# V stage: the low parts of the gates of 30 of 32 quads subtracted on GpSimd, between its gathers

## What is computed

```python
def block(args):
    xb, eb, gb = args
    u = jnp.take(u_tab, eb, axis=0)
    act = jax.nn.gelu(jnp.einsum("cd,ced->ce", xb, u))
    vv = jnp.take(v_tab, eb, axis=0)
    return jnp.einsum("ce,ced->cd", gb * act, vv)
```

## Time and profile before

| what | value |
|---|---|
| median of 3 runs | 1966.7 us (1954.4 to 1967.1) |
| the profiled execution | 1962.9 us |
| its span, first to last instruction | 1961.1 us |
| busy PE, DVE, ACT, POOL | 97%, 80%, 49%, 27% of the span |
| V stage, first to last dense matmul | 1471.3 to 1949.6 us |
| VectorE's loop with gathers, first to last | 1482.4 to 1945.9 us |

### The profile page before, as it was taken

One profiled execution on the slowest core, in us unless ns is written; L12 is line 12 of the kernel. 1 busy time (PEld: TensorE's weight loads), 2 busy tenths in 40 slices (PEclk: granted clock), 3 DMA queues, 4 the chain that ended last, 5 costly groups with the idle time before them and its releaser, 6 DMA issues.

```text
span 1961.1 us, 34213 instructions
## 1 busy us (share of the span) xinstructions
PE 1906.1 (97%) x13424; PEld 1678.9 (86%) x13424; DVE 1561.5 (80%) x2398; ACT 965.0 (49%) x1387; POOL 525.1 (27%) x511
## 2 busy tenths in 40 slices
PE   8999999999999999999999999999999999999997
PEld 7887877777788888888888888888999999998886
DVE  6758575667544999997868878756988999999998
ACT  5535453565544444445444444445774544444444
POOL 0000000000000000000012222203777777877774
PEclk9999999999999999999999999999999999999999
DMA  7523333236655556555578888856989999999997
GB/s 242 194 84 123 90 117 98 66 116 213 205 186 171 186 191 193 187 190 193 188 223 285 282 276 282 282 190 212 320 267 351 395 386 390 383 387 386 387 396 276
DMA packets 151775, 470.32 MB, mean 240 GB/s; under 512 B 20192, under 2 KB 47872, under 8 KB 151104
## 3 DMA queue, kind: packets, MB, share of 16 engines
q1 hardware_dynamic: 118064, 331.23, 50.6%
q0 software_dynamic: 33552, 136.90, 18.7%
HBM read 438.63 MB, written 29.43 MB: 239 GB/s over the span
## 4 chain that ended last, share of the span: by engine, by line
PE 78%; DVE 11%; DMA 4%; issue 3%; ACT 3%; DVEq 0%; SPq 0%; ACTq 0%
PE ps L1782 78%; DVE sums L1109 3%; DMA vraw<-in_peer_v 2%; DVE lo L1101 2%; ACT hi L690 1%; DMA raw<-in_w_out 0%; DMA raw<-in_wq 0%; DMA got<-in_peer_v,row_ids 0%; DVE vlo L1642 0%; DVE a_lo L1698 0%; DVE zt L1199 0%; DVE xc L1109 0%; DVE hT L1109 0%; DMA oneJ<-oneJ_spill 0%; DVE TmTT L1334 0%
## 5 line engine op out<-in xcount | busy, mean ns | idle before, releaser
L1782 PE MATMUL ps<-hT,hi 128*128 128x512 f32 x2992 | 1065.7, 400 | 7.6 <-DVE lo L1101 7.6
L1782 PE MATMUL ps<-hT,lo 128*128 128x256 f32 x2992 | 839.3, 281 | 0.0
L1782 PEld LDWEIGHTS ps<-hT,hi 128*128 128x128 f32 x2992 | 563.0, 188 | 142.0 <-issue 9.2
L1101 DVE TENSOR_TENSOR lo<-raw,hi 128x1024 fp32r<-128x1024 f32 x406 | 492.0, 1223 | 197.7 <-ACT hi L690 192.9
L690 ACT ACTIVATE hi<-raw 128x1024 fp32r<-128x1024 f32 x406 | 423.5, 1060 | 420.6 <-DMA raw<-in_peer_u 370.8
L1782 PEld LDWEIGHTS ps<-hT,lo 128*128 128x128 f32 x2992 | 566.9, 189 | 0.1
L648 POOL DMA_INDIRECT got<-in_peer_v,row_ids x256 | 353.7, 1382 | 109.8 <-DVE sums L1109 73.0
L975 ACT ACTIVATE vhi<-vraw 128x896 fp32r<-128x896 f32 (+1 forms) x256 | 194.3, 766 | 250.7 <-DMA vraw<-in_peer_v 224.3
L1782 PE MATMUL ps<-vhi,a_hi 128*128 128x448 f32 x768 | 240.5, 368 | 6.9 <-DVE vlo L1642 4.9
L1109 DVE SCALAR_TENSOR_TENSOR sums<-got,wT,sums 128x704 f32<-128x704 f32 x256 | 243.8, 952 | 2.8 <-DMA got<-in_peer_v,row_ids 2.2
L1782 PE MATMUL ps<-vlo,a_hi 128*128 128x448 f32 x768 | 239.8, 367 | 0.0
(11 more groups left out here) (292 smaller groups left out, 1829.6 us busy)
## 6 DMA issues: line engine op xcount, KB each, us to landing
raw<-in_peer_u SPq DMA_DIRECT2D x256, 512.0 KB, 3.5
vraw<-in_peer_v SPq DMA_DIRECT2D x124, 448.0 KB
raw<-in_w_in SPq DMA_DIRECT2D x86, 512.0 KB, 3.5
vraw<-in_peer_v SPq DMA_DIRECT2D x124, 224.0 KB
raw<-in_w_out SPq DMA_DIRECT2D x32, 512.0 KB, 3.6
raw<-in_wq SPq DMA_DIRECT2D x32, 512.0 KB, 3.5
oneJ_spill<-madeJ POOLq DMA_DIRECT2D x64, 256.0 KB, 5.0
oneJ<-oneJ_spill SPq DMA_DIRECT2D x64, 256.0 KB, 4.9
```

The source lines that it names most:

```text
L1101: V.tensor_tensor(lo[n % NR][:, :], raw[n % NR][:, :], hi[n % NR][:, :].bitcast(F32), ALU.subtract).then_inc(lo_done, 1)
L1782: return nc.tensor.matmul(o, lhsT, rhs, start=start, stop=stop, skip_group_check=True)
```

## The change

`act_lo` of the quads 2 to 31 moves from VectorE's loop into POOL's loop of gathers. It stands before `gather(k)` where k % 8 is 6, for the quad k // 8 + 1. It waits for `ahi_done`, and counts itself in `oneG_made` behind the 64 that are there. TensorE waits for `alo_done` for the first two quads and for `oneG_made` from tile 8 on. The DMAs `xr` and `gf` wait on the new counter, with the numbers moved accordingly. The instruction itself is the same: 128 x 1024, `Zq` minus `a_hi`, into `a_lo`.

```diff
+            def act_lo(q):
+
+                pool.wait_ge(sem("ahi_done"), 4 + q)
+                nc.gpsimd.tensor_tensor(
+                    a_lo[q % 2][:, :, :].rearrange("p k (g t) -> p k g t", t=TOK4),
+                    Zq[:, q].rearrange("p t k -> p (t k)").rearrange("p (g k t) -> p k g t", k=4, t=TOK4),
+                    a_hi[q % 2][:, :, :].bitcast(F32).rearrange("p k (g t) -> p k g t", t=TOK4),
+                    ALU.subtract).then_inc(sem("oneG_made"), 1)
+
             for k in range(NT2 * PICKS):
+                if k % 8 == 6 and 2 <= k // 8 + 1 < N_QUAD:
+                    act_lo(k // 8 + 1)
                 gather(k)
                 if k >= 128 and k % 8 == 0 and k < 192:
                     q = (k - 128) // 8
-                    pool.wait_ge(sem("alo_done"), 6 + q // 2)
+                    pool.wait_ge(sem("oneG_made"), N_TOK4 + 1 + q // 2)
...
-                    pool.wait_ge(sem("alo_done"), 11)
+                    pool.wait_ge(sem("oneG_made"), N_TOK4 + 6)
...
                 v_lo(k)
                 done = k - 2 * V_HIS
-                if done % 8 == 7 and done // 8 + 2 < N_QUAD:
-                    act_lo(done // 8 + 2)
...
             for i in range(N_V - 1):
-                pe.wait_ge(sem("alo_done"), i + 1 if i < 4 else 4 + i // 4)
+                if i < 8:
+                    pe.wait_ge(sem("alo_done"), i + 1 if i < 4 else 5)
+                else:
+                    pe.wait_ge(sem("oneG_made"), N_TOK4 + i // 4 - 1)
```

## The result

The changed kernel takes 2006.7 us (median of 4 runs, 2005.5 to 2008.9), the kernel before 1966.2 (4 runs). The ratio is 1.0217, with an interval from 1.0199 to 1.0235: slower by 2.2%. The prediction had the sign of its likeliest case right and the size wrong: 1979 was forecast, 2005 was the top of the range.

What follows compares the result with a forecast made beforehand. PE was taken to bound the kernel, with VectorE becoming the bound: +9 us for its load, +3 for remaining idle time, +3.5 for gathers, +15.5 on 1962.9, 1978.4, given as 1979; range 1961 to 2005.

Steps and rivals of the forecast that it cites:

- its likeliest case: VectorE's loop with gathers: VectorE stopped 1.85 us per subtraction and becomes the bound, 1966 to 1990 us; chance 0.60.
- What bounds the kernel: Loop with gathers: PE sets the pace, busy 458.4 of 463.5 us, and can give back at most 5.1 us.
- Rival B: Loop with gathers: PE stays the bound, exclusion costs VectorE less than the 34 us relieved; 1958 to 1966 us; chance 0.14.
- The exclusion: VectorE's loop: each GpSimd subtraction reading SBUF stops VectorE for 1.85 us, 30 times, 55.5 us in all.
- My 0.21: Amount in us by which a VectorE stop was taken to be shorter than the GpSimd instruction's span: 2.06 - 0.21 = 1.85.
- VectorE's term: VectorE's loop: 55.5 us of standing still for 34 us of work removed, +21.5 us, need 472.5.
- The waits for gathers: VectorE's loop: delayed gathers mostly hidden by the queue, 3.5 us in all, bounds 0 and 42.
- The parking that I read at quad 28: GpSimd's queue, late quads: GpSimd stands 6.9 us for `a_hi`, and the next gather misses its use by 3 us.
- Rival C: Late quads: GpSimd parks on `a_hi` and gathers starve VectorE, 21 us on top, 1996 us; chance 0.18.
- TensorE: TensorE's wait for low parts from GpSimd: margin about zero at quad 3, 0 to 1 us for a few early quads.

Runs made afterwards that it cites:

- e1_none: Kernel before with the low parts of quads 2 to 31 left out altogether: 1961.6 us, ratio 0.9987.
- e10_psum_pool: e4_follow with VectorE's additions of gathers run in PSUM, so each reads one tensor in SBUF: 1984.3 us.
- e4_follow: Changed kernel with each subtraction placed later by the extra picks done so far, so GpSimd never reaches it before `a_hi` is made: 1996.0 us.
- e2_memset: Changed kernel with GpSimd clearing `a_lo` twice instead of subtracting, same place and wait, no read of SBUF: 1973.5 us.
- e6_one_input: e4_follow with GpSimd multiplying `a_hi` by 0 into `a_lo` instead of subtracting, one SBUF input instead of two: 1994.7 us.
- e8_memset_follow: e2_memset with its clearing instructions at the later place of e4_follow, so neither SBUF reads nor parking on `a_hi`: 1967.7 us.
- e9_psum_dve: Kernel before with VectorE's additions of gathers run in PSUM, low parts staying on VectorE: 1963.0 us.

## Why the prediction was wrong

**What bounds the kernel: right.** PE sets the pace and gives back nearly nothing: e1_none has 1961.6, not told apart from before. Rival B is out, since VectorE isn't relieved.

**The exclusion: right, and its size too small.** It was read from four instructions of the trace. I took 1.85 us a stop, from a span of 2.06 scaled up from 128 x 512 and less 0.21. The subtraction lasts 2.36 us undisturbed (e10_psum_pool), and the stop is 2.09 us in the changed kernel and 2.4 in e4_follow and e10_psum_pool: the whole of the instruction, with nothing to take off. My 0.21 was read from a product of GpSimd that had itself been held: it began 0.16 us behind a `v_lo` and ended 0.90 us behind that one's end (1465.80 to 1466.70), and the `v_lo` that waited for it waited for that rest, not for a whole product. VectorE's term is +29 us where +21.5 was forecast, 8 us of the miss. The rule in the Trainium skill (SBUF — State Buffer, "Who interferes with whom"), that the one that comes second is blocked for the whole instruction of the other, agrees with these runs better than my 0.21 did: 2.4 of 2.36 to 2.48 us. The same page exempts a GpSimd instruction that only writes and, outside the two-port modes, a VectorE instruction with one SBUF input; e2_memset and the additions of e10_psum_pool agree. One run doesn't fit the "whole instruction": in e6_one_input a multiplication of 2.8 us holds VectorE for 1.1, and a `v_lo` at 1539.28 lasts its usual 1.08 us while the multiplication (1537.54 to 1540.35) is still recorded as running.

**The waits for gathers: the step that failed.** I wrote that "A delay of 3 us makes the queue shorter, not the landing later" and took 3.5 us in all, "near the low end", because "ACT is further ahead" when VectorE is the bound. Measured are 28.1 us, and VectorE's idle time rose by 18.5 us where I had it fall by 6: 25 us, the larger part of the miss. (With the 8 us above that is 32 us for the loop; the time is off by 28, since the loop began 4 us earlier.) Both halves of the argument were off. The parking that I read at quad 28 came about (14.2 us, six times, from quad 23 on) and cost 11 us by e4_follow; ACT was not far enough ahead. Of the 28.1 us, 19.6 fall behind the 160th addition, in that part of the loop. And without parking, e8_memset_follow still has 18.6 us of waits for 1.9 us of GpSimd once in eight gathers: the six buffers were not deep enough to hide it. Rival C, the starved VectorE at 1996, named this mechanism and got 0.18; it gave the waits 21 us on top of the forecast, and the stops were larger too.

**How they add up.** Late gathers alone, with the 30 us of subtractions gone from VectorE, are nearly harmless (e8_memset_follow: 0.3% over before), and stops with few late gathers cost 33 us (e4_follow). In the changed kernel VectorE was the bound by its stops, so that each us of waiting went to the end.

**TensorE: right.** Up to 1600 us its matmuls wait for `v_lo` alone, 4.8 us in eight pieces of at most 0.8, and never for a subtraction.

## What to carry to other kernels

Work that leaves a full engine for an idle one is no relief if the two can't read at the same time: here 1.13 us on VectorE became a stop of 2.1 to 2.4. First ask what the removal alone would bring, by a kernel that leaves the work out; here that was nothing. And a queue that issues transfers in a tight rotation of buffers may have no idle time to give away though it is seen waiting: here GpSimd stood 73 us waiting for buffers, and 1.9 us put into its queue once in eight gathers brought VectorE 18.6 us of waits.

## What the runs showed that was not expected

- The engine that starts first in the record isn't always the one that goes first. The addition at 1540.64 began 0.39 us before the subtraction and was held through all of it. The same order of starts stands in 8 of the 30 stops of the changed kernel and in 29 of 30 in e10_psum_pool.
- An instruction of GpSimd with one input, multiply by a constant, lasts 2.8 us for 128 x 1024 and is slower than a subtraction of two tensors (2.36); clearing the same tile takes 0.97. It held VectorE for 1.1 us only. Why, no run here tells.
- When the additions run in PSUM and the subtraction in quarters, a gather occupies GpSimd for 1.07 us in the mean after 1.38 in the kernel before. The traces show that gathers, too, wait for VectorE's reads. In the kernel before, 235 of 250 gathers end 0.80 to 0.86 us behind the end of a VectorE instruction with two tensors in SBUF, and the other 15 last under 1.0 us. "One stop" above has such a case: the addition ends at 1544.14, the gather at 1544.97. An addition in PSUM has no such effect: in e9_psum_dve all 250 gathers follow the same rule with the splits and subtractions alone. No run was made for this by itself.
